# Reading a layer's sorted rows back on ScalarE's queue ahead of its first silu

## What is computed

```
for i in range(DEPTH):                       # 4 layers
    y = mixer_i(h)
    h = layer_norm(DN_ALPHA * h + y, ln_mix_g[i], ln_mix_b[i])
    m = grouped_moe(h, ...)
    h = layer_norm(DN_ALPHA * h + m, ln_ffn_g[i], ln_ffn_b[i])

# grouped_moe: 16 experts in 4 groups, 2 experts for each token, from one group
out = zeros
for e in range(N_EXPERTS):                   # 16
    h = silu(t @ w1[e]) * (t @ w3[e])        # 1024 -> 512
    out = out + gates[:, e:e+1] * (h @ w2[e])  # 512 -> 1024
```

## Time and profile before

| | |
|---|---|
| median of 3 runs | 1867.17 us (1866.41 to 1870.75) |
| the profiled execution's own time | 1866.66 us |
| its span | 1864.6 us |
| granted TensorE clock, mean | 0.961 |
| TensorE matmuls busy | 1704.0 us (91%) |
| VectorE, ScalarE, GpSimd busy | 661.2, 456.3, 164.9 us |
| moved by the transfers | 521.86 MB, mean 280 GB/s |
| share of queue q1 (SP) of the 16 transfer engines' time | 65.9% |
| share of q10 (ScalarE), q0 (GpSimd) | 2.3%, 1.1% |

### The profile page before, as it was taken

The page is one execution under the profiler, slowest core; times in us unless marked ns, Lnnn a source line. Parts: engine busy times, 40 slices in busy tenths (PEclk is TensorE's granted clock), DMA queues, the critical chain, the costliest instruction groups (busy, mean ns, idle before and its releaser), DMA issues. The chain is left out here.

```text
span 1864.6 us, 24338 instructions
## 1 busy us (share of the span) xinstructions
PE 1704.0 (91%) x9154; PEld 887.3 (48%) x9154; DVE 661.2 (35%) x1397; ACT 456.3 (24%) x898; POOL 164.9 (9%) x129
## 2 busy tenths in 40 slices
PE   8998979998898888899999997899999998799986
PEld 7866643332584443333344544333368667433322
DVE  3443563221306562232302225222243435542223
ACT  2573312111204121111211101111124834121111
POOL 1013110000300100000020100000030131200000
PEclk9999989999999889999999998999999999899998
DMA  9531089999943289689963339899993220699995
GB/s 335 184 122 47 24 329 425 425 426 426 373 143 131 83 368 425 275 346 426 402 251 144 113 150 376 352 426 426 424 353 136 91 92 2 265 387 425 426 425 218
DMA packets 91034, 521.86 MB, mean 280 GB/s; under 512 B 9027, under 2 KB 17268, under 8 KB 63996
## 3 DMA queue, kind: packets, MB, share of 16 engines
q1 hardware_dynamic: 77552, 497.04, 65.9%
q10 hardware_dynamic: 11020, 14.07, 2.3%
q0 software_dynamic: 2304, 8.39, 1.1%
HBM read 510.03 MB, written 9.45 MB: 279 GB/s over the span
## 5 line engine op out<-in xcount | busy, mean ns | idle before, releaser
L2106 PE MATMUL bank<-ring,work 128*64 128x512 f32 x1280 | 369.7, 599 | 7.9 <-issue 7.9
L1614 DVE TENSOR_TENSOR work<-bank,work 64x512 f32<-64x512 f32 x64 | 67.9, 1061 | 538.0 <-ACT work L1022 537.9
L1771 PE MATMUL bank<-HT,ring 128*128 128x256 f32 x1024 | 232.8, 388 | 0.0
L1771 PEld LDWEIGHTS bank<-HT,ring 128*128 128x128 f32 x1024 | 199.4, 195 | 37.4 <-issue 10.2
L2106 PEld LDWEIGHTS bank<-ring,work 128*64 128x64 f32 x1280 | 115.0, 138 | 195.3 <-issue 192.9
L2150 PE MATMUL bank<-ring,work 128*64 128x512 f32 x896 | 203.7, 598 | 2.5 <-issue 2.5
L1779 PE MATMUL bank<-ring,HT 128*128 128x512 f32 x448 | 198.3, 602 | 0.0
L2106 PE MATMUL bank<-early_slot,work 128*64 128x512 f32 x320 | 143.9, 603 | 9.6 <-issue 9.6
L2106 PE MATMUL bank<-work 128*64 128x512 f32 x320 | 145.3, 604 | 5.2 <-issue 5.2
L1022 ACT ACTIVATE work<-bank 64x512 f32<-64x512 f32 x64 | 37.7, 589 | 441.9 <-PE bank L2106 441.9
L1779 PEld LDWEIGHTS bank<-ring,HT 128*128 128x128 f32 x448 | 85.8, 194 | 104.1 <-issue 104.1
(11 more groups left out here) (318 smaller groups left out, 1824.9 us busy)
## 6 DMA issues: line engine op xcount, KB each, us to landing
ring<-in_e_w SPq DMA_DIRECT2D x136, 2048.0 KB, 20.0
early_slot<-in_e_w SPq DMA_DIRECT2D x20, 2048.0 KB, 18.1
work<-in_e_w SPq DMA_DIRECT2D x20, 2048.0 KB, 22.6
ring<-in_a_w_in SPq DMA_DIRECT2D x15, 2048.0 KB, 19.7
HT<-in_e_w SPq DMA_DIRECT2D x16, 1024.0 KB, 19.7
work<-in_e_w SPq DMA_DIRECT2D x16, 1024.0 KB, 17.7
ring<-in_c_w_in SPq DMA_DIRECT2D x8, 2048.0 KB, 21.7
ring<-in_b_w_in SPq DMA_DIRECT2D x6, 2048.0 KB, 25.3
```

The source lines that it names most:

```text
L1614: v.tensor_tensor(by_m(h_[j]), bank[b][CAP:, :], sil[j][CAP:, :], ALU.mult).then_inc(drained[b], 1)
L1771: ins = mm(dst[:, 0:SEQ], wt[:, k, n * P:(n + 1) * P], HT[:, k, :], start=k == 0, stop=k == KC - 1)
L2106: ins = mm(bank[b][lo:lo + CAP, :], x[:, k, :], wt[k], start=k == 0, stop=k == KC - 1, skip_group_check=True)
```

## The change

SP loses its wait for the scatter and the four reads of the sorted rows. ScalarE gets both, in front of the lead pair, ahead of its reads of the experts' counts and of the first silu. The reads, their sizes, their buffers and what waits for them stay the same. SP's next entry in its list is then the first freed ring slot.

```diff
--- before.py
+++ after.py
@@ -555,18 +555,11 @@
 
             for tt in range(TT):
                 sp.dma_start(H[:, tt, :], w["x"][0, tt * P:(tt + 1) * P, :]).then_inc(x_ready[tt], 16)
-            brought = 0
             halves_key = {key[0]: key for key, src, slot, after in loads if slot == HALVES and after[0] == "gathered"}
             for key, src, slot, after in loads:
                 if key == 1:
 
                     sp.wait_ge(rows_for_cols, N_ROWS)
-                if after is not None and after[0] == "moe" and after[1] == brought:
-
-                    sp.wait_ge(rows_out, 16 * 2 * TT * (brought + 1))
-                    for c in range(4):
-                        sp.dma_start(xr[c], choice_rows[c * P:(c + 1) * P, :]).then_inc(rows_back, 16)
-                    brought += 1
                 if after is not None:
                     release(after)
                 elif slot == LATE:
@@ -1048,6 +1041,9 @@
                             ins = a(y_[CAP * j:CAP * (j + 1), nh * 512:(nh + 1) * 512], bank[b][nh * CAP:(nh + 1) * CAP, :], ACT.Copy)
                         ins.then_inc(drained[b], 1)
 
+                act.wait_ge(rows_out, 16 * 2 * TT * (i + 1))
+                for c in range(4):
+                    act.dma_start(xr[c], choice_rows[c * P:(c + 1) * P, :]).then_inc(rows_back, 16)
                 pair(0, True)
                 with act.Fori(1, E // 2) as it:
                     pair(it, False)
```

## The result

The changed kernel takes 1901.11 us at the median (1893.87 to 1909.49, 4 runs), the kernel before 1867.1 us in the same comparison: a ratio of 1.0164, 95% interval 1.0134 to 1.0193. It is slower, by some 31 to 34 us where 47.7 us were forecast. The time lies just under the forecast's own range (1902 to 1926 us) and inside the whole range (1884 to 1930 us). The profiled execution took 1897.58 us.

What follows compares the result with a forecast made beforehand. The weight stream bounds the ends of layers 0 and 3, TensorE those of layers 1 and 2. Layer costs 0 + 17.8 + 16.1 + 13.8 = 47.7 us on 1866.66 give 1914.4 us; own range 1902 to 1926, whole range 1884 to 1930 us.

Steps and rivals of the forecast that it cites:

- Rival A: The move is harmless, only the silu's path costs, 3.0 us in layer 1: about 1869.5 us, chance 0.09.
- B: The two queues share by equal bytes, rows at 212 GB/s, layers 1 and 2 late by 5.7 and 5.3 us: near 1878 us, chance 0.05.
- the silu's delay: ScalarE's wait and four issues precede the first silu; alone, 3.0 us in layer 1, with layers 0 and 3 absorbing theirs.
- rival C: The scatter lands sooner in layers 1 and 3, whose cost falls to near nothing; layer 2's stays: about 1884 us, chance 0.08.
- 425 GB/s from its first experts on: Layers 0 and 3 were said to stream at 425 or 426 GB/s from their first experts on.
- 13.5 us to spare: End of layer 0 waits for the weight stream, so TensorE's 6.5 us lateness there is absorbed: cost 0.
- rival D: Layer 0 is hit too if its row reads slip by 3 us: 13.8 us more, 1928 us, chance 0.08.
- the dry stream: Layer 3: the weight queue empties while TensorE waits; 14.1 us idle, less 0.3 for the earlier start: 13.8 us.
- the rows' head start: Layer 1: rows move alone for 1.17 us, 0.5 MB, then 1.6 MB beside the weights need 18.8 us.
- TensorE bounds layer 1: After layer 1's dip the stream follows TensorE's releases, so its 17.8 us delay reaches the layer's end in full.
- two more when TensorE begins the turn of h, some 7 to 11 us later: Two further ring loads follow the first two without a gap, 8.4 MB; layer 2's rows finish with them, 24.7 us.
- the two bounds: ScalarE's register reads ahead of the first silu, bounded by zero and a second 1.28 us; the upper end was taken.

Runs made afterwards that it cites:

- after_silu: The changed kernel with ScalarE's wait and its four row reads moved from in front of the first silu to right behind it: 1932.06 us, ratio 1.0307.

## Why the prediction was right, and where its sizes were off

**The mechanism.** It held: one packet for one (40 to 39), the rows last to arrive, TensorE idle ahead of the transposes, a weight stream that runs dry in layer 3. Rival A falls with the result, and with the runs in which the queues are kept apart; B with the packets' sizes; the silu's delay, which I had priced at 3.0 us, measures 2.5 by the stages (by the ratio 6, 1 to 11). The measured time lies between the forecast and rival C, but C's condition did not occur: the reads were issued 8.1, 10.6, 13.9 and 12.4 us after the first scatter, where it was 8.1, 10.5, 14.1 and 12.7 before. Three layers each lost less than forecast, and the sum was 15.5 us too large. Two slips of the prediction changed nothing: layer 3 does not show 425 GB/s from its first experts on, has 387 in the slice from 1632 us; and rival B's 5.7 us in layer 1 come out at 6.5 by its own terms.

**Layer 0: 0 forecast, -1.3 measured.** The rows landed 13.2 us after the first issue (14.2 forecast), TensorE was late by 4.6 us (6.5), and its 13.5 us to spare took it. `after_silu` shows rival D's condition made on purpose: 3 us later reads, 15 us at the end of the layer (13.8 forecast).

**Layer 3: 13.8 forecast, 11.2 measured.** Landing 27.6 us after issue (28.3 forecast), first down product 18.8 us late (20.7), and the end goes by the dry stream, as worked out: in 1678 to 1688 us the transfer engines are busy for 2.1 us of 10.

**Layer 1: 17.8 forecast, 12.5 measured.** The mis-sized term is the rows' head start. I let the ring loads start moving as long after their issue as the rows after theirs, and gave the rows 1.2 us alone. The packets by queue in 674:676 (one line), 676:678 (two), and in layer 2 in 1150:1152 (one) and 1152:1154 us (its q10):

```profile
q10 hardware_dynamic: 204, 0.77, 98.0%
...
q10 hardware_dynamic: 107, 0.38, 64.8%
q1 hardware_dynamic: 20, 0.33, 39.1%
...
q1 hardware_dynamic: 45, 0.74, 88.7%
...
q10 hardware_dynamic: 10, 0.04, 5.0%
```

The ring loads issued at 673.51 have none in 674 to 676 and 20 in the next 2 us; the rows of layer 2, issued at 1149.98 behind ring loads, have none before 1152. In steps of half a us, the first packets of these two pass in 676.5 to 677 and in 1153.5 to 1154, those of layer 1's rows, issued at 672.52 on idle engines, in 673 to 673.5. Whoever comes second starts about 3.5 us after issue, whoever finds the engines idle about 1 us. The rows of layer 1 had moved 1 MB by then, 0.77 of it in 674 to 676 alone, and not 0.5. 0.5 MB at 85 GB/s is 6 us; the landing came 4.5 us earlier than worked out, 19.4 us after the first issue and not 23.9. The shorter transposes (5.0 us, 6.29 taken) are the other microsecond. Layer 1's end moved by as much as its first down product, +12.3 and +12.2 in the first profiles: the step "TensorE bounds layer 1" held.

**Layer 2: 16.1 forecast, 9.8 measured.** The step that failed is "two more when TensorE begins the turn of h, some 7 to 11 us later". The silu was 7.5 us late, the last four matmuls of `up` waited 3.06 us for VectorE's product, and TensorE then stood 5.40 us more ahead of the turn, so that the turn began 15.6 us after the first ring load. By then the first two loads, 9.9 us of stream, were through, and the rows had the engines nearly to themselves: 129 of their packets to 32 in 1160 to 1162 us, 225 to 1 in the next two. `after_silu`, where the turn is on time, gives the forecast's 16.2. What held TensorE for those 5.40 us no row names. It stands in layer 2 of all seven profiles in which the silu is late (2.5 to 5.5 us), is 1.80 us in `after_silu` and absent in the kernel before. Instruction packets of 16 KB pass at 1160 to 1161 and 1164 to 1165 us, so a late fetch of code would fit; that is argued, not shown. The end moved by more than the first down product there (+10.0 against +6.9 in the first profiles), since the last pair waits for weights in both kernels, and longer in the changed one: its first silu comes 21.4 us after the last one of the pair ahead of it, before 17.0 and 20.1 in the two profiles, where TensorE's own pace is 14.4. I had taken that for a shift without a loss.

**The silus** came at the forecast places, the delays 1.8, 4.0, 7.5 and 5.5 us against 1.5, 3.9, 8.5 and 5.9. For layers 0 to 3:

```profile
269.18 0.59 ACT L1015 ACTIVATE work<-bank 64x512 f32<-64x512 f32 x1
...
675.41 1.28 ACT L1015 ACT_TABLE_LOAD   x1 [22.43 <-issue]
676.71 0.59 ACT L1015 ACTIVATE work<-bank 64x512 f32<-64x512 f32 x1
...
1154.33 0.59 ACT L1015 ACTIVATE work<-bank 64x512 f32<-64x512 f32 x1
...
1658.35 0.59 ACT L1015 ACTIVATE work<-bank 64x512 f32<-64x512 f32 x1
```

The table load of layer 1 begins 1.1 us after the last of four issues ends and takes 1.28 us; the register reads lie between the two bounds.

## What to carry to other kernels

A transfer moved to another engine's queue loses its place in line: it competes packet by packet, and what counts is the packets' sizes on both sides. In this kernel a read with small packets that the next step waits for was best on the queue of the large-packet stream, ahead of it; on the other queue, larger packets or holding the stream back until it had landed won only a part back. Before moving one, look at what else will be on the wire in the microseconds after its issue, and at which layer or stage has slack for it.

## What the runs showed of the hardware

The Trainium skill (DMA: Bandwidth & Descriptors, "Queues, rings and completion order") says that each engine goes round the queues it has work for, a packet at a time, with a packet of some 9 to 17 descriptors. The runs agree on the round; how many descriptors a packet has, no run here shows. The turn goes by the packets that the trace counts: 16 KB of a weight, 2, 4 or 12 KB of the rows, whichever a partition's contiguous run is (46 to 47, 40 to 39, 31 to 32).

A transfer that comes second on another queue starts about 3.5 us after issue, against about 1 us on idle engines, in either direction: in the changed kernel the ring loads of layers 0 and 1 start 3 to 3.7 us after issue behind the rows, and the rows of layers 2 and 3, behind the ring loads, 3.5 to 4 us after issue.

The kernel before has a spread of its own. Two profiles of it, 1540 to 1550 us, in layer 3's DeltaNet stage; first the first one:

```profile
1540.00:1550.00 10.00, 8.34 (x172) 7.66 (x170) 5.15 (x11) 6.50 (x18) 2.84 (x3) 1.00 0.01 3
```

And the second:

```profile
1540.00:1550.00 10.00, 10.00 (x72) 9.12 (x69) 2.47 (x4) 2.86 (x8) 0.00 (x0) 0.50 0.01 2
```

A granted clock of 1.00 in one and of 0.50, the lower level, in the other, though TensorE is busy through all of the second stretch. The second profile is some 4 us behind the first there, so the windows do not hold quite the same work; over the same 30 us of the stage, from 1530 us in the first profile, the granted clocks by steps of 10 us are 0.83, 1.00 and 1.00 against 0.63, 0.68 and 0.83. The stage took 259.4 and 266.8 us. Three of the experiments' profiles show the lower level there too, with 266 to 267 us. The passes of layer 1 for more than 64 rows vary likewise: between the silus of pair 2's two experts 26.3 and 26.0 us in the two profiles of before, 24.7 and 24.6 in the changed kernel's, 29.3 in that with 12 KB packets. Medians of the kernel before went from 1867 to 1874 us in four comparisons, so differences below some 5 us were read from the stages and not from totals.
